# Earlier first norm, pieces split ahead, and another order of work at 17 stage boundaries

## The reference

```python
def first_block(x, ...):                     # 2 layers
    # layer 0: x += sparse attention (compressed, selected, window)(rms_norm(x))
    # layer 1: x += block attention(rms_norm(x)), keys and values from rms_norm(x, kv_norm)
    # each layer: x += hier_moe(rms_norm(x))             32 experts, width 128, top 2 of one group
    #             g = sigmoid(rms_norm(x) @ ple_w_gate[i])
    #             x += g * (P[i] @ ple_w_proj[i])        "embedding" stage

def second_block(x, c, ...):                 # 4 layers
    for i in range(4):
        shift, scale, gate = (silu(c) @ ada_w[i] + ada_b[i]) ...
        x = x + 0.5 * gate[0] * swiglu(adaln(x, ...), ffn_w_in[i, 0], ffn_w_out[i, 0])
        x = x + gate[1] * mixer_i(adaln(x, ...))         # rwkv7, mamba2, window attention, rwkv7
        x = x + 0.5 * gate[2] * swiglu(adaln(x, ...), ffn_w_in[i, 1], ffn_w_out[i, 1])
```

## Time and profile before

| | us |
|---|---|
| median of 3 runs | 3949.12 (3946.58 to 3949.45) |
| the profiled execution, its span | 3952.3, 3950.5 |
| PE busy | 3660.7 (93%) |
| DVE, ACT, POOL busy | 2587.0, 1797.9, 430.2 |
| mean granted TensorE clock | 0.958 of 2.4 GHz |

### The profile page before, as it was taken

The page is one execution under the profiler, slowest core; times in us unless marked ns, Lnnn a source line. Parts: engine busy times, 40 slices in busy tenths (PEclk is TensorE's granted clock), DMA queues, the critical chain, the costliest instruction groups (busy, mean ns, idle before and its releaser), DMA issues.

```text
span 3950.5 us, 51736 instructions
## 1 busy us (share of the span) xinstructions
PE 3660.7 (93%) x19842; PEld 3007.2 (76%) x19842; DVE 2587.0 (65%) x4865; ACT 1797.9 (46%) x3151; POOL 430.2 (11%) x365
## 2 busy tenths in 40 slices
PE   6999988999899789989998989999989998999899
PEld 6767877688678767768787967878868787777687
DVE  4567764667676665567777776777567777665554
ACT  3254453634554443354546645454454544433343
POOL 2000002100000421100002420000000002322100
PEclk9899998999999899989999999999999999899999
DMA  5126852278567220058683426868338684200153
GB/s 230 54 75 245 283 185 101 101 261 280 181 225 276 95 73 1 1 189 304 222 299 144 143 78 204 302 226 294 138 117 300 227 301 154 100 28 1 59 181 107
DMA packets 181650, 670.13 MB, mean 170 GB/s; under 512 B 31264, under 2 KB 31776, under 8 KB 173216
## 3 DMA queue, kind: packets, MB, share of 16 engines
q1 hardware_dynamic: 181408, 666.83, 47.9%
HBM read 665.66 MB, written 1.10 MB: 169 GB/s over the span
## 4 chain that ended last, share of the span: by engine, by line
PE 80%; DVE 12%; ACT 5%; issue 2%; POOL 1%; DMA 0%; SPq 0%; DVEq 0%; ACTq 0%; POOLq 0%
PE pb L273 76%; PE pb L280 5%; ACT wp L264 2%; DVE wp L226 2%; DVE wk L238 2%; DVE wk L226 2%; DVE sq L238 1%; ACT wk L264 1%; DVE hx L226 1%; DVE sq L226 1%; DVE hT L233 0%; ACT sq L264 0%; POOL wp L226 0%; DVE xt L226 0%; DMA ring<-weights 0%
## 5 line engine op out<-in xcount | busy, mean ns | idle before, releaser
L273 PE MATMUL pb<-wp,hx 128*128 128x512 f32 (+1 forms) x6432 | 1591.2, 400 | 42.8 <-DVE hx L226 40.9
L273 PEld LDWEIGHTS pb<-wp,hx 128*128 128x128 f32 x6432 | 1213.9, 193 | 292.2 <-DVE hx L226 24.6
L226 DVE TENSOR_TENSOR wp<-ring,wp 128x1024 fp32r<-128x1024 f32 (+1 forms) x903 | 1057.8, 1203 | 548.7 <-ACT wp L264 546.7
L264 ACT ACTIVATE wp<-ring 128x1024 fp32r<-128x1024 f32 x936 | 959.5, 1054 | 684.8 <-PE pb L273 658.6
L273 PE MATMUL pb<-wp,ex 128*128 128x512 f32 x2928 | 706.0, 391 | 1.0
L273 PEld LDWEIGHTS pb<-wp,ex 128*128 128x128 f32 x2928 | 548.2, 188 | 123.6 <-issue 5.0
L226 POOL TENSOR_TENSOR wp<-ring,wp 128x512 fp32r<-128x512 f32 (+1 forms) x123 | 234.9, 1914 | 2678.8 <-ACT wp L264 2678.7
L264 ACT ACTIVATE wk<-pb 128x256 f32<-128x256 f32 (+4 forms) x604 | 261.1, 437 | 384.2 <-PE pb L273 209.7
L273 PE MATMUL pb<-wk 128*128 128x128 f32 (+8 forms) x3008 | 388.2, 293 | 21.3 <-ACT wk L264 6.6
L273 PEld LDWEIGHTS pb<-wk 128*128 128x128 f32 (+4 forms) x3008 | 286.7, 172 | 114.8 <-issue 45.4
L273 PE MATMUL pb<-hx,wp 128*128 128x256 f32 x2688 | 345.6, 289 | 22.6 <-DVE hx L226 12.0
(11 more groups left out here) (176 smaller groups left out, 2750.6 us busy)
## 6 DMA issues: line engine op xcount, KB each, us to landing
ring<-weights SPq DMA_DIRECT2D x1088, 512.0 KB, 5.3
ring<-weights SPq DMA_DIRECT2D x35, 1536.0 KB, 6.6
ring<-weights SPq DMA_DIRECT2D x24, 1024.0 KB, 5.0
cst<-gate_rows SPq DMA_DIRECT2D x12, 512.0 KB, 5.3
cst<-consts SPq DMA_DIRECT2D x1, 1984.0 KB, 10.6
ring<-weights SPq DMA_DIRECT2D x1, 1280.0 KB, 5.3
ring<-weights SPq DMA_DIRECT2D x1, 1152.0 KB, 5.3
xt<-x_in SPq DMA_DIRECT2D x1, 1024.0 KB, 4.8
```

What stands on the lines that cost most here:

```text
L226: return self.real.tensor_tensor(out, a, b, op) if self.real else Uncounted()
L264: return self.real.activation(out, a, func, bias=bias, scale=scale, accum_out=accum)
L273: return self.real.matmul(out, l, r, start=start, stop=stop, skip_group_check=skip)
```

## The change

The loads of `x`, the parameters and the constants get a semaphore each (`s_x`, `s_p`, `s_in`), and the engines wait for what they need next. The first stage does its norm, both tiles step by step together, ahead of the splits of its first weights. A feed-forward stage has two more pieces split in the boundary before it (`fifth`, the first two of pair 1, low parts by POOL), PE does 15 repeated products behind the transposes of tile 0 (ahead of `gate_up(0)`), and the first four feature blocks of `gate_up(2)` (tile 0) go between the transposes of tile 1 and `gate_up(1)`. An embedding stage ends tile by tile: gate and projection of tile 0, gate of tile 1, transposes of tile 0, projection of tile 1. At boundaries into other stages than feed-forward and embedding (`by_tile` false), DVE does the update (1, 1) ahead of `halves_dve(0)`, and ACT squares tile 1 within `halves_act(0)`.

```diff
-    BEHIND_NORM = 17
+    BEHIND_NORM, BEHIND_TURN = 17, 15
...
+            self.by_tile, self.fifth = gated_units, []
...
-        def halves_act(self, e, t):
+        def halves_act(self, e, t, between=()):
+                    if n == 0 and k == 2:
+                        for step in between:
+                            step()
...
         for t in range(2):
             for hf in range(2):
                 h.square_act(e, t, hf)
+        for t in range(2):
             h.root_act(e, t)
             h.unit_act(e, t)
+        for t in range(2):
             h.halves_act(e, t)
 
     def first_head_dve(e):
         h = head_of(0)
         for t in range(2):
             h.var_dve(e, t)
+        for t in range(2):
             h.root_dve(e, t)
+        for t in range(2):
             h.halves_dve(e, t)
 
-    def boundary_act(e, st, pieces=None, middle=()):
+    def boundary_act(e, st, pieces=None, middle=(), second=()):
         h, now = head_of(st + 1), early(st + 1)
         split_hi(e, now[:2] if pieces is None else pieces)
         for step in middle:
             step()
         if h is None:
             return
+        now = [p for p in now if p not in h.fifth]
         e.tables("natural_log_exp_and_others")
         split_hi(e, now[2:3])
         h.square_act(e, 0, 0)
-        split_hi(e, now[3:])
+        split_hi(e, now[3:] if not second else [])
         h.square_act(e, 0, 1)
         h.root_act(e, 0)
         h.unit_act(e, 0)
-        h.halves_act(e, 0)
-        for hf in range(2):
-            h.square_act(e, 1, hf)
+        for step in second:
+            step()
+        squares = [lambda hf=hf: h.square_act(e, 1, hf) for hf in range(2)]
+        h.halves_act(e, 0, () if h.by_tile else squares)
+        split_hi(e, now[3:] if second else [])
+        for step in squares if h.by_tile else ():
+            step()
+        split_hi(e, h.fifth[:1])
         h.root_act(e, 1)
         h.unit_act(e, 1)
         if h.gated_units:
             e.tables("silu_and_others")
+        split_hi(e, h.fifth[1:])
         h.halves_act(e, 1)
 
     def boundary_dve(e, st, update, order, pieces=None, middle=()):
...
             h.root_dve(e, 0)
         if (1, 0) not in before:
             update(1, 0)
-        if h is not None:
+        if h is not None and h.by_tile:
             h.halves_dve(e, 0)
         update(1, 1)
         if h is not None:
+            if not h.by_tile:
+                h.halves_dve(e, 0)
             split_lo_v(e, now[3:])
             h.var_dve(e, 1)
             h.root_dve(e, 1)
         g.gu.append([])
-        g.first = gate_up(0, 0, 4)
+        g.first, g.fifth = gate_up(0, 0, 4), []
+        if not routed:
+            g.gu.append([])
+            g.fifth = gate_up(1, 0, 2, "g")
         for p in range(P):
-            if p + 1 < P:
+            if p + 1 < P and len(g.gu) == p + 1:
                 g.gu.append([])
             if gate is not None and p == P // 2:
                 plan_gate(st, *gate)
...
-            b = gate_up(p + 1, 0, 2) if more else []
+            b = gate_up(p + 1, 0, 2) if more and not (p == 0 and g.fifth) else []
...
-        def gate_up(s, between={}):
+        def gate_up(s, between={}, blocks=range(KD), warm=0):
             p, t = divmod(s, 2)
             key = (st, "glu", s)
-            ps = bk.hold(e, 4 + s % 3, key, (v_out, key))
-            for k in range(KD):
+            ps = bk.hold(e, 4 + s % 3, key, (v_out, key)) if blocks[0] == 0 else pb[4 + s % 3]
+            repeated_pe(e, ps, warm)
+            for k in blocks:
                 w = g.gu[p][k // 2]
                 split_ready(e, w)
                 e.wait_ge(*x_lo[st, "h", t, k])
             whole_down(2)
             whole_down(3)
         else:
-            gate_up(0, second_tokens)
+            gate_up(0, second_tokens, warm=BEHIND_TURN)
+            gate_up(2, {}, range(0, 4))
             gate_up(1, {6: lambda: turn(0)})
-        for s in range(6 if g.routed else 2, last):
+            gate_up(2, {7: lambda: turn(1)}, range(4, KD))
+            whole_down(0)
+        for s in range(6 if g.routed else 3, last):
             gate_up(s, {6: lambda: turn(s - 1)})
             whole_down(s - 2)
         gate_up(last, {1: lambda: turn(last - 1)})
...
+            first_head_dve(e)
+            e.wait_ge(s_in, 16)
-            first_head_dve(e)
...
+            first_head_act(e)
-            first_head_act(e)
+            e.wait_ge(s_in, 16)
+            for a in (0, 32):
+                e.act(both_rows[a:a + 32, :], ident[a:a + 32, a:a + 32], ACT.Copy).then_inc(*a_step.up("rows"))
+            e.act(both_rows[64:128, :], ident[64:128, 0:32], ACT.Copy).then_inc(*a_step.up("rows"))
+            e.act(both_cw[64:128, :], C("S384")[64:128, 0:256], ACT.Copy, scale=0.0).then_inc(*a_step.up("rows"))
...
-        S.first = G_.first
+        S.first, S.head.fifth = G_.first + G_.fifth, G_.fifth
+        S.head.by_tile = True
...
                 proj(0, t)
-            for t in range(2):
-                gate(1, t)
-            for t in range(2):
-                proj(1, t)
+            gate(1, 0)
+            proj(1, 0)
+            gate(1, 1)
             boundary_pe(e, st)
+            proj(1, 1)
 
         def outs():
...
             groups = outs()
+
+            def gates_open(t, hf):
+                e.wait_ge(*product[st, "gate", t, hf])
+                e.act(XS[:, t, hf * 512:(hf + 1) * 512], pb[4 + 2 * hf + t][:, :], ACT.Sigmoid).then_inc(
+                    *a_out.up((st, "gate", t, hf)))
+
             for n, g in enumerate(groups):
                 split_hi(e, g.due)
                 if n == 1:
                     e.wait_ge(*landed(c_p))
                     e.act(ph, pT, ACT.Copy).then_inc(*x_hi.up((st, "p")))
-                if n in (4, len(groups) - 1):
-                    hf = n // 5
+                if n == 4:
                     for t in range(2):
-                        e.wait_ge(*product[st, "gate", t, hf])
-                        e.act(XS[:, t, hf * 512:(hf + 1) * 512], pb[4 + 2 * hf + t][:, :], ACT.Sigmoid).then_inc(
-                            *a_out.up((st, "gate", t, hf)))
-            boundary_act(e, st)
+                        gates_open(t, 0)
+            boundary_act(e, st, None, [lambda: gates_open(0, 1)], [lambda: gates_open(1, 1)])
 
         def pool(e):
...
-        e.wait_ge(s_in, 48)
+        e.wait_ge(s_p, 16)
+        e.wait_ge(s_in, 16)
-        e.wait_ge(s_in, 48)
-        e.fill(eps[:, 0:1], 1e-6).then_inc(*v_step.up())
-        e.fill(eps[:, 1:2], -0.5e-6).then_inc(*v_step.up("eps"))
+        e.fill(eps[:, 0:1], 1e-6).then_inc(*v_step.up("eps"))
+        e.wait_ge(s_x, 16)
+        e.fill(eps[:, 1:2], -0.5e-6).then_inc(*x_new.up(*[(-1, t, hf) for t in range(2) for hf in range(2)]))
-            e.fill(selw[64:128, k * 16 + 2 * k + 1:k * 16 + 2 * k + 2], 1.0).then_inc(
-                *x_new.up(*[(-1, t, hf) for t in range(2) for hf in range(2)]))
+            e.fill(selw[64:128, k * 16 + 2 * k + 1:k * 16 + 2 * k + 2], 1.0).then_inc(*v_step.up())
+        e.wait_ge(s_p, 16)
-        e.wait_ge(s_in, 48)
-        for a in (0, 32):
-            e.act(both_rows[a:a + 32, :], ident[a:a + 32, a:a + 32], ACT.Copy).then_inc(*a_step.up("rows"))
-        e.act(both_rows[64:128, :], ident[64:128, 0:32], ACT.Copy).then_inc(*a_step.up("rows"))
-        e.act(both_cw[64:128, :], C("S384")[64:128, 0:256], ACT.Copy, scale=0.0).then_inc(*a_step.up("rows"))
+        e.wait_ge(s_p, 16)
-        e.wait_ge(s_in, 48)
+        e.wait_ge(s_x, 16)
+        e.wait_ge(s_p, 16)
+        e.wait_ge(s_in, 16)
-        e.dma(xt[:, :], d_x).then_inc(s_in, 16)
-        e.dma(prm[:, :], d_p).then_inc(s_in, 16)
+        e.dma(xt[:, :], d_x).then_inc(s_x, 16)
+        e.dma(prm[:, :], d_p).then_inc(s_p, 16)
...
```

More of the change, by code:

```diff
@@ L366, in build_program @@
     s_in, s_out, s_c, s_gate = (ctx.enter_context(nc.semaphore(n)) for n in ("s_in", "s_out", "s_c", "s_gate"))
+    s_x, s_p = (ctx.enter_context(nc.semaphore(n)) for n in ("s_x", "s_p"))
     s_ring = [ctx.enter_context(nc.semaphore(f"s_ring{i}")) for i in range(NLAND)]
```

## The result

The changed kernel took 3919.2 us (median of 4, 3914.9 to 3925.8), the kernel before 3949.3 on the same chip: ratio 0.9927, interval 0.9909 to 0.9944. That is 30 us faster, where 46.4 were forecast. The time lies in the range (3889 to 3924), but beyond the forecast's own range (3891 to 3914), and on the rival "the feed-forward entries give nothing" (3920).

What follows compares the result with a forecast made beforehand. PE was taken as the bound (80% of the chain of waits), losing time to useless products, low clock and waits. Six terms summed to 46.4 us off 3952.3, less 3.2 for the median, giving 3903 us; range 3889 to 3924.

Steps and rivals of the forecast that it cites:

- the feed-forward entries give nothing: Rival: at feed-forward entries the sixth piece arrives after the repeated products have done their harm; 3920 us, chance 0.20.
- The first norm: Start of the kernel: norm ahead of the first weights' splits, PE's first product at 24.3 instead of 37.32; 11.7 us gained.
- The 1.3 taken off for the clock: At the start: 1.3 us subtracted from a 13.0 us lead for a clock falling while PE waits for the first piece.
- The rival that the lead is lost in stage 0: Stage 0, pieces coming through three slots: the first norm's lead is lost again; 3915 us, chance 0.09 for lost or late.
- Embedding stage 2: Embedding stage 2 into block attention: tile 1's transposes at 617.5 instead of 626.49; 9.0 us gained.
- two table loads: Tile 1's norm after embedding stage 2: one load hidden, a second between logarithm and exponential; 9.0 us gained, 10.3 with one.
- Embedding stage 5: Embedding stage 5 into feed-forward stage 6: same order, `gate_up(1)` starts at 1095.6 against an equal point of 1106.6; 10.3 us gained.
- Entries from mixers (part 4): Entries into stages 8, 11, 14, 17: earlier clock rise and `gate_up(1)` without a gap; 2.7 us each, 10.8 gained.
- the fifth and sixth low parts are there at 1725.4 and 1729.6: Stage 8's entry, standing for four: both low parts ready before PE needs them at 1728.9 and 1730.3, so no wait.
- Entries from feed-forward (part 5): Entries into stages 9, 12, 15: 0.4, 0.4 and 0.9 us, 1.7 gained; bounds -5 and 6.
- Update (1, 1) first (part 6): Boundaries into rwkv, mamba, window attention and experts: 2.8 + 1.7 - 1.6, 2.9 us gained; bounds -4 and 7.
- a loss of 0.8 each: Experts stages 1 and 4: two squares ahead of the last high parts make the logits wait, 0.8 us lost each.

Runs made afterwards that it cites:

- only_embed: The kernel before with only the embedding stages ending tile by tile (stage 3 keeps the changed order of update (1, 1)): 3931.7 us, ratio 0.9965.
- no_repeat: The changed kernel without the 15 repeated products: 3915.3 us, ratio 0.9932.
- dve_no_repeat: The changed kernel with fifth and sixth low parts by DVE, ACT's splits of them moved earlier, and no repeated products: 3895.8 us, ratio 0.9875.
- only_order: The kernel before with only update (1, 1) ahead of tile 0's halves and tile 1's squares within them: 3945.2 us, ratio 1.0001.
- early_pool: The changed kernel with ACT's splits of the fifth and sixth piece between tile 1's squares and ahead of the silu table, low parts still by POOL: 3904.5 us, ratio 0.9886.

## Why the prediction was right and wrong

The forecast's sign of being wrong, PE waiting for `wp` of POOL at all eight entries, came true. The time lies in the range only because the range reached down to that rival.

- **The first norm: right.** 11.7 forecast, 12.2 alone (7.1 to 17.4); by the trace of the changed kernel stage 1's logits start at 261.73 instead of 274.46, 12.7 earlier. The lead was 14.0 at the first product (13.0 in the sum: ACT was 0.6 us earlier, and the first low part took 2.36 us and not 2.82). The 1.3 taken off for the clock was lost too, but elsewhere: the granted clock was 0.50 for 20.5 us from 107.4, where it had been for 17.1 from 123.3, and 1.00 in the wait for the first piece. That this term came out is luck. The rival that the lead is lost in stage 0 is refuted.
- **Embedding stage 2: right, and two table loads right.** From tile 0's transposes of stage 2 to tile 1's of stage 3 it is 59.9 us before, 50.7 in `only_embed` (9.2 gained, 9.0 forecast) and 47.9 in the changed kernel, where the second tile's gate ran in 5.73 us at the full clock. Of the 9.2 of `only_embed` 3.2 went back to the clock in stage 4. The second load does lie between logarithm and exponential. The Trainium skill (ScalarE: Activation LUTs, "Table sets: the hidden batching unit") would have one load here, since one set holds both functions; the trace has 597.75 and 599.36, and only asking for that set by name made it one. The kernel has 55 table loads instead of 50, where four more were forecast.
- **Embedding stage 5: right.** From tile 0's transposes of stage 5 to the first hidden transposes of stage 6, 59.0 us instead of 70.6 (with the 2.8 added): 11.6, where 10.3 was forecast. In the second trace of the same kernel it is 63.2, so 7.4 gained; the granted clock over the stretch was 0.97 in the one and 0.89 in the other. PE waited 2.63 for the sixth piece (2.3 forecast), and 1.02 for the transposes, where the sum had nothing.
- **Entries from mixers (part 4): wrong, 4.5 instead of 10.8.** The repeated products end 7.2 us behind the transposes' start (7.0 forecast) and `gate_up(0)` 12.7 (12.7). The step that failed is "the fifth and sixth low parts are there at 1725.4 and 1729.6", which is 14.4 behind the transposes: the sixth was there at 16.1, and PE waited 1.28 where no wait was forecast. That it was 1.6 us later fits the 1.8 by which DVE's operation was held: ACT waits for it (idle 2.35 in stage 9) ahead of the scaling, the silu table and the split. No run takes this alone away. With DVE's low parts and ACT's other places stage 8 takes 20.9 against 24.0 before, 3.1 gained for the 2.7 recorded. Stage 8 also didn't stand for the four: stage 11 gained nothing.
- **Entries from feed-forward (part 5): wrong, 5.3 lost instead of 1.7 gained, beyond the bound of -5.** The same step: the sixth was 2.58 late instead of 1.45, with 0.78 of idle time ahead of the transposes besides. And `gate_up(0)` at the full clock gave back no more than the repeated products took (`no_repeat`, `dve_no_repeat`).
- **Update (1, 1) first (part 6): right in the idle stretches, wrong in the experts stages.** The idle time is 6.20 instead of 7.19 us into 10 and 13, 3.9 and 4.3 instead of 5.47 into 7 and 16: 4.8 gained, where 4.5 was forecast. The step that failed is "a loss of 0.8 each" in the experts stages. `only_order` lost 2.7 in each: the sum had no term for the clock behind the new wait. 4.8 - 5.4 agrees with what the part was worth alone, -0.4 us (-3.9 to 3.2).

The step at fault in parts 4 and 5 has one root: the sums let POOL's splits run beside DVE at no cost to DVE. I weighed the rule of the Trainium skill (SBUF — State Buffer, "Who interferes with whom") for POOL's split at the start, found it not borne out by a mean of two, and dropped it for the whole sum. What it says of the other side, that a DVE instruction with two SBUF inputs is kept out while GpSimd reads, is what happened in stages 8, 9, 11, 12, 14, 15 and 17: 2.03 instead of 0.22 us, over at POOL's end, and 3.36 instead of 1.22 in `early_pool`.

The mean was a misreading, and the trace of the kernel before shows the hold in both directions. These are its rows 3 one by one, and the root's correction at the boundary into stage 10, beside the very POOL operation of rows 10:

```profile
17.23 2.35 POOL L226 TENSOR_TENSOR wp<-ring,wp 128x1024 fp32r<-128x1024 f32 x1 [16.80 <-ACT wp L264]
18.06 2.60 DVE L226 TENSOR_TENSOR wp<-ring,wp 128x1024 fp32r<-128x1024 f32 x1 [3.10 <-ACT wp L264]
19.53 3.34 POOL L226 TENSOR_TENSOR wp<-ring,wp 128x1024 fp32r<-128x1024 f32 x1
2103.50 0.42 DVE L238 SCALAR_TENSOR_TENSOR stat<-stat 128x1 f32<-128x1 f32 x1 [0.41 <-ACT stat L264]
```

POOL's first split took its usual time and DVE's, which began within it, 2.60 us instead of 1.23; then POOL's second waited for DVE and took 3.34. The root took 0.42 us instead of 0.22 and ended at 2103.92, where POOL ended at 2103.91. So the price could have been read before: an instruction that is held waits until the other one ends, and the new POOL splits would lie beside the norm of tile 1.

I gave "the entries give nothing" 0.20 and wrote beside it that a late sixth piece, "last on ACT and then on POOL", would be its cause. That late piece decided it, and the held root made it later than my own sums had it.

Open: why the clock falls in one placing of a stretch and not in another; and 7 us between the sum of the parts and the whole, which the intervals cover.

## What to carry to other kernels

Before work is given to an idle GpSimd, list which DVE instructions with two SBUF inputs will run beside it, and look for one in a chain that somebody waits for: its size doesn't matter here, since a 128x1 operation lasted to the end of the 128x1024 one beside it. Read such rows one by one, not as a mean: 2.35 and 3.34 us show a hold that 2.82 hides. When filler or early work is put ahead of a product, check first that no later input is late, or the time only moves into the next wait. A change that only shifts work in time can lose or win 3 us of clock at places it doesn't touch, so compare by stage and not only by totals.

## What of the hardware was not expected

- DVE's 128x1 operation with both inputs in SBUF took 2.03 us beside a 2.39 us operation of POOL, and 0.22 without it. DVE's reads from PSUM (four of 128x128, 1.36 us) are as long beside POOL, at the end of stage 8's entry, as without it; the `hx` split behind them, which has two SBUF inputs, took 1.48 instead of 0.42.
- The same 24 products behind the same idle time took 5.72 us in one kernel and 7.98 in another.
- 15 repeated products of 3.3 us at 2.4 GHz, or 5.2 where they start at 1.2, returned as much as they cost and no more. 7 did better than both 15 and none over the seven entries, mostly at those from mixers; in stages 9 and 15 the entry took the same 17.5 us with 7 and with none.
